# Four-row operands for small fp32 matmuls, and small steps spread between half chunks

## The reference

```
# block 1: feed-forward, then a mixer with q/k normalisation, rotary tables and attention, then feed-forward
x = x + 0.5 * ml[2] * swiglu(modulate(rms_norm(x, norm1_g), ml[0], ml[1]), ffn1_w_in, ffn1_w_out)
bg, cg, vc, q, k, v, gt = split(modulate(rms_norm(x, norm2_g), ml[3], ml[4]) @ w_in)     # the same for ctx
q, k = rms_norm(q per head, q_norm_g), rms_norm(k per head, k_norm_g)   # 8 q heads, 2 k/v heads of 128
q, k = apply_axial_rope(q), apply_axial_rope(k)                         # the 256 latent tokens
o = softmax(q @ k_all.T * 128 ** -0.5) @ v_all                          # 512 keys: 256 ctx, 256 latent
x = x + ml[5] * merge_branches(conv_branch(bg, cg, vc), o, gt, w_branch_conv, w_branch_attn, w_out)
x = x + 0.5 * ml[8] * swiglu(...); x = rms_norm(x, final_g)
# block 2, layer 0: an mLSTM of 4 heads of 256 (input and forget gates from h @ 8 columns of w_in_ab) and
# a stick-breaking attention of 8 heads of 128; layer 1: pooled windows. Each with w_in, w_out and norms.
b = cumsum(lf); W = exp(b[t] - b[s] + ic[s] - m_t); h = num / max(|den|, exp(-m_t))
```

## Time and profile before

| | |
|---|---|
| median of 3 runs | 1343.05 us (1342.46 to 1348.6) |
| profiled execution, its own time | 1343.05 us |
| its span in the trace | 1341.0 us |
| PE busy | 1304.0 us, 97% of the span |
| PE weight load (PEld) busy | 1205.3 us |
| VectorE (DVE) busy | 905.2 us, 68% |
| ScalarE (ACT) busy | 647.3 us, 48% |
| mean granted TensorE clock | 0.988 |

### The profile page before, as it was taken

How to read it: one execution, slowest core, us unless ns; L and a number is a source line. 1 busy time by engine, 2 the same in 40 slices (tenths; PEclk the granted TensorE clock), 3 DMA queues, 4 the chain that set the end, 5 groups by cost and what they waited for, 6 DMA issues and landing times. The chain is left out here.

```text
span 1341.0 us, 23443 instructions
## 1 busy us (share of the span) xinstructions
PE 1304.0 (97%) x9310; PEld 1205.3 (90%) x9310; DVE 905.2 (68%) x1462; ACT 647.3 (48%) x1025; POOL 31.4 (2%) x32
## 2 busy tenths in 40 slices
PE   5999999999999999999999999999999999999996
PEld 3688888888889999999999999989999999999996
DVE  3577875556558587755775555788887666689863
ACT  4432222222336335545465445666666765556552
POOL 0000000000020000000010000200000000100000
PEclk6999999999999999999999999999999999999998
DMA  8746556464554345444546665556555454447550
GB/s 306 261 159 202 190 189 217 160 234 161 191 182 142 111 131 168 130 149 138 181 143 193 201 194 178 165 172 176 152 152 166 133 188 152 142 129 219 188 174 32
DMA packets 201404, 229.68 MB, mean 171 GB/s; under 512 B 7120, under 2 KB 191696, under 8 KB 201296
## 3 DMA queue, kind: packets, MB, share of 16 engines
q1 hardware_dynamic: 201008, 227.90, 53.4%
q10 hardware_dynamic: 288, 0.28, 0.1%
HBM read 227.10 MB, written 1.05 MB: 170 GB/s over the span
## 5 line engine op out<-in xcount | busy, mean ns | idle before, releaser
L1038 PE MATMUL P<-XHB,WH 128*128 128x256 f32 (+1 forms) x1808 | 553.6, 306 | 7.6 <-DVE XLB L1683 3.7
L1039 PE MATMUL P<-XLB,WH 128*128 128x256 f32 (+1 forms) x1808 | 543.7, 301 | 0.0
L1040 PE MATMUL P<-XHB,WL 128*128 128x256 f32 (+1 forms) x1808 | 543.6, 301 | 0.0
L1871 DVE TENSOR_TENSOR WL<-W,WH 128x1024 fp32r<-128x1024 f32 x358 | 431.9, 1224 | 96.4 <-ACT WH L1466 96.1
L1466 ACT ACTIVATE WH<-W 128x1024 fp32r<-128x1024 f32 x358 | 369.1, 1042 | 247.2 <-PE P L1040 169.9
L1038 PEld LDWEIGHTS P<-XHB,WH 128*128 128x128 f32 x1808 | 340.6, 188 | 28.1 <-issue 7.3
L1039 PEld LDWEIGHTS P<-XLB,WH 128*128 128x128 f32 x1808 | 340.4, 188 | 15.4 <-issue 0.5
L1040 PEld LDWEIGHTS P<-XHB,WL 128*128 128x128 f32 x1808 | 340.6, 188 | 14.8
L1038 PE MATMUL P<-GH,WH 128*128 128x256 f32 (+1 forms) x372 | 121.2, 326 | 0.0
L1040 PE MATMUL P<-GH,WL 128*128 128x256 f32 (+1 forms) x372 | 120.6, 324 | 0.0
L1039 PE MATMUL P<-GL,WH 128*128 128x256 f32 (+1 forms) x372 | 120.6, 324 | 0.0
(11 more groups left out here) (305 smaller groups left out, 1811.9 us busy)
## 6 DMA issues: line engine op xcount, KB each, us to landing
W<-in_ffn_w_in SPq DMA_DIRECT2D x88, 512.0 KB, 4.9
W<-in_w_in_ab SPq DMA_DIRECT2D x72, 512.0 KB, 4.6
W<-in_w_modt SPq DMA_DIRECT2D x56, 512.0 KB, 4.0
W<-in_w_in SPq DMA_DIRECT2D x52, 512.0 KB, 3.9
W<-in_ffn_w_out SPq DMA_DIRECT2D x40, 512.0 KB, 4.7
W<-in_w_in_c SPq DMA_DIRECT2D x32, 512.0 KB, 4.3
W<-in_w_mod SPq DMA_DIRECT2D x16, 512.0 KB, 7.2
W<-in_w_out_ab SPq DMA_DIRECT2D x16, 512.0 KB, 4.4
```

The source lines that it names most:

```text
L1038: pe.matmul(o, h[:, k, c], xh[:, kk, a:b], start=kk == 0, stop=False)
L1039: pe.matmul(o, h[:, k, c], xl[:, kk, a:b], start=False, stop=False)
L1040: mm = pe.matmul(o, l[:, k, c], xh[:, kk, a:b], start=False, stop=kk == gm.nk - 1)
L1871: dve.tensor_tensor(l, a, h.bitcast(F32), ALU.subtract).then_inc(S["wl"], 1)
```

## The change

It changes the shapes of some small fp32 operands and the order of some small steps.

- Shapes: HOT is replaced by a constant `hot` of 16 columns; "qa" uses 4 columns of it (128 rows by 4 columns) and writes 4 PSUM rows; root and reciprocal work on 4 partitions. "qb" and the two `sel` matmuls of "m0" take 4 rows of `sel` and 4 rows of the moving operand. G has 4 partitions.
- GpSimd's three memsets and the semaphores `hot` and `gz`, with the waits on them, are gone.
- Order: in `qk_norm`, "qb" of tile i comes first, then a yield, then "rope" of the tile before and a yield. In `attention`, "score", "gather" and "turn" no longer stand in one tick but have a yield between them, and ScalarE's exponential is done in the "score" step, ahead of the "gather" and "turn" copies, with no step of its own.

```
-for _name, _n in (("id", 128), ("one", 128), ("eps", 1), ("ee", 1), ("gat", 2), ("cnt", 26), ("perm", 128),
+for _name, _n in (("id", 128), ("one", 128), ("eps", 1), ("ee", 1), ("hot", 16), ("gat", 2), ("cnt", 26), ("perm", 128),
...
         for i in range(4):
+            b, f = self.bank(self.up("qn"))
+            self.step("qb", a=s, b=i, c=self.at("qn"), bank=b, free=f)
+            at = self.at("qn")
+            yield
             if todo is not None:
                 self.rope(*todo)
+                yield
                 todo = None
-            b, f = self.bank(self.up("qn"))
-            self.step("qb", a=s, b=i, c=self.at("qn"), bank=b, free=f)
             if s < 2 or i % 2:
-                todo = (s, i, self.at("qn"))
+                todo = (s, i, at)
...
-            yield
-            yield
...
         score(0)
-        self.step("exp", a=0, bank=4 + (self.uses - 1) % 3)
         for i in range(16):
-            for _ in range(2):
-                yield
+            yield
+            yield
             self.step("scale", a=i)
-            for _ in range(2):
-                yield
             if i + 1 < 16:
                 while missing(i + 1):
                     yield True
                 score(i + 1)
-                bank = 4 + (self.uses - 1) % 3
+            yield
             if i and i % 2 == 0:
                 b, f = self.bank(self.up("ol"))
                 self.step("gather", a=i // 2 - 1, bank=b, free=f)
+            yield
             b, f = self.bank(self.up("at"))
             self.step("turn", a=i, bank=b, free=f)
-            if i + 1 < 16:
-                self.step("exp", a=i + 1, bank=bank)
-        for _ in range(2):
+        for _ in range(3):
             yield
...
-            G = sbuf(st, "G", [128, 6, T])
+            G = sbuf(st, "G", [4, 6, T])
...
-                        pe.matmul(ps[:, 0:T], HOT[:, 3 - i:131 - i], SQ[...], start=i == 0,
+                        pe.matmul(ps[0:4, 0:T], con("hot", 4 * i, 4 * i + 4), SQ[...], start=i == 0,
...
-                    pe.matmul(ps[:, 0:T], con("sel", 128 * s.b, 128 * s.b + 128),
+                    pe.matmul(ps[:, 0:T], con("sel", 128 * s.b, 128 * s.b + 128, 4),
                               rows_of(s.a), start=True, stop=True).then_inc(S["qb"], 1)
...
-                    pe.matmul(ps[:, 0:T], con("sel", 128 * h, 128 * h + 128), G[:, 4, 0:T], start=True, stop=True)
-                    pe.matmul(ps[:, T:2 * T], con("sel", 128 * h, 128 * h + 128), G[:, 5, 0:T], start=True,
+                    pe.matmul(ps[:, 0:T], con("sel", 128 * h, 128 * h + 128, 4), G[:, 4, 0:T], start=True, stop=True)
+                    pe.matmul(ps[:, T:2 * T], con("sel", 128 * h, 128 * h + 128, 4), G[:, 5, 0:T], start=True,
                               stop=True).then_inc(S["m1p"], 1)
...
-            pool.wait_ge(S["md"], 56)
-            pool.memset(HOT, 0.0).then_inc(S["hot"], 1)
-            pool.wait_ge(S["hot"], 1)
-            pool.memset(HOT[:, 3:4], 1.0).then_inc(S["hot"], 1)
...
-                if name == "s3":
-                    pool.wait_ge(S["oh"], 8)
-                    pool.memset(G[:, 4:6, :], 0.0).then_inc(S["gz"], 1)
...
-                    act.activation(rows_of(s.a), ps[:, 0:T], ACT.Sqrt, scale=1.0 / 128, bias=con("eps")) \
+                    act.activation(rows_of(s.a), ps[0:4, 0:T], ACT.Sqrt, scale=1.0 / 128, bias=con("eps", rows=4)) \
...
-                elif s.kind == "exp":
+                elif s.kind == "score":
                     i = s.a
                     act.wait_ge(S["am2"], i + 1)
...
-                    dve.wait_ge(S["gz"], 1)
```

More of the change, by code:

```diff
@@ L78, in constants @@
     put("ee", np.full((128, 1), EPS * EPS, np.float32))
+    hot = np.zeros((128, 4, 4), np.float32)
+    for i in range(4):
+        hot[:, i, i] = 1.0
+    put("hot", hot.reshape(128, 16))
     put("gat", (p[:, None] % 32 == np.arange(2)[None, :]).astype(np.float32))
@@ L712, in qk_norm @@
         for i in range(4):
+            b, f = self.bank(self.up("qn"))
+            self.step("qb", a=s, b=i, c=self.at("qn"), bank=b, free=f)
+            at = self.at("qn")
+            yield
             if todo is not None:
                 self.rope(*todo)
+                yield
                 todo = None
-            b, f = self.bank(self.up("qn"))
-            self.step("qb", a=s, b=i, c=self.at("qn"), bank=b, free=f)
             if s < 2 or i % 2:
-                todo = (s, i, self.at("qn"))
+                todo = (s, i, at)
             else:
                 self.ready.add(self.name(s, i))
-                self.end[self.name(s, i)] = self.at("qn")
-            yield
-            yield
+                self.end[self.name(s, i)] = at
         if todo is not None:
@@ L845, in build_program @@
         seq, stat, end = plan.seq, plan.stat, plan.end
-        names = ("g wh wl zero gz hot sc mm mr mt mv md cb sf sq pa on sr ra ri rb am gm out sil1 hm1 hh1 hl1 xu1 sil2 hm2 hh2 hl2 xu2 "
+        names = ("g wh wl zero sc mm mr mt mv md cb sf sq pa on sr ra ri rb am gm out sil1 hm1 hh1 hl1 xu1 sil2 hm2 hh2 hl2 xu2 "
                  "nt nh nl xh xr rx "
@@ L900, in build_program @@
             SM = sbuf(st, "SM", [128, 4, 4])
-        HOT = MC[:, 0, 0:131]
         with ExitStack() as st:
@@ L948, in rows_of @@
         def rows_of(s):
-            return MC[:, 7, :] if s == 2 else RS[:, 1, T * s:T * s + T]
+            return MC[0:4, 7, :] if s == 2 else RS[0:4, 1, T * s:T * s + T]
         def head(s, i):
@@ L1121, in _ @@
                 elif s.kind == "qa":
-                    pe.wait_ge(S["hot"], 2)
                     for i in range(4):
@@ L1125, in _ @@
                         pe.wait_ge(S["qs"], n + 1)
-                        pe.matmul(ps[:, 0:T], HOT[:, 3 - i:131 - i], SQ[:, n % 3, T * (n // 3 % 2):T * (n // 3 % 2) + T], start=i == 0,
+                        pe.matmul(ps[0:4, 0:T], con("hot", 4 * i, 4 * i + 4), SQ[:, n % 3, T * (n // 3 % 2):T * (n // 3 % 2) + T], start=i == 0,
                                   stop=i == 3).then_inc(S["qh"], 1)
@@ L1175, in _ @@
                     for j in range(2):
-                        mm = pe.transpose(ps[:, 4 * j:4 * j + 4], G[0:4, 2, 128 * j:128 + 128 * j], con("id", 0, 4, 4))
+                        mm = pe.transpose(ps[:, 4 * j:4 * j + 4], G[:, 2, 128 * j:128 + 128 * j], con("id", 0, 4, 4))
                     mm.then_inc(S["gmm"], 1)
@@ L1570, in _ @@
                 elif s.kind == "g1":
-                    t2 = G[0:4, 2, 0:T]
+                    t2 = G[:, 2, 0:T]
                     act.wait_ge(S["gfree"], 1)
-                    act.activation(t2, G[0:4, 1, 0:T], ACT.Abs).then_inc(S["gab"], 1)
+                    act.activation(t2, G[:, 1, 0:T], ACT.Abs).then_inc(S["gab"], 1)
                     act.wait_ge(S["gab"], 1)
@@ L2073, in _ @@
                     dve.wait_ge(S["gr0"], 1)
-                    dve.tensor_scalar(G[0:4, 0, 0:T], TS[0:4, 5, 0:T], V[0:4, VEC["bi"][0]:VEC["bi"][1]], None, ALU.add) \
+                    dve.tensor_scalar(G[:, 0, 0:T], TS[0:4, 5, 0:T], V[0:4, VEC["bi"][0]:VEC["bi"][1]], None, ALU.add) \
                         .then_inc(S["gr0"], 1)
@@ L2077, in _ @@
                     dve.wait_ge(S["gmm"], 1)
-                    dve.tensor_scalar(G[0:4, 1, 0:T], ps[0:4, T:2 * T], V[0:4, VEC["bf"][0]:VEC["bf"][1]], None, ALU.add) \
+                    dve.tensor_scalar(G[:, 1, 0:T], ps[0:4, T:2 * T], V[0:4, VEC["bf"][0]:VEC["bf"][1]], None, ALU.add) \
                         .then_inc(S["gfree"], 1)
                 elif s.kind == "g2":
-                    ig, b, t2, top, neg = (G[0:4, i, 0:T] for i in range(5))
+                    ig, b, t2, top, neg = (G[:, i, 0:T] for i in range(5))
                     dve.wait_ge(S["gfree"], 1)
@@ L2099, in _ @@
                     dve.wait_ge(S["dv"], own)
-                    dve.tensor_tensor(G[0:4, 5, 0:T], neg, b, ALU.subtract).then_inc(S["gq"], 1)
+                    dve.tensor_tensor(G[:, 5, 0:T], neg, b, ALU.subtract).then_inc(S["gq"], 1)
                 elif s.kind == "g4":
```

## The result

| | before | after |
|---|---|---|
| median of 11 runs each, in turn on one chip | 1348.05 us | 1357.49 us |
| lowest and highest | 1341.86, 1355.03 | 1349.24, 1362.73 |
| profiled execution, its own time | 1343.05 | 1357.65 |
| its span | 1341.0 | 1355.9 |

The ratio is 1.0067, with a 95% interval of 1.0043 to 1.0092, or +5.8 to +12.4 us. The forecast was a ratio of 1349.0/1343.05 = 1.0044, at the lower edge of that. The time lies above the range of 1342.5 to 1353.0. The runs of either kernel scatter over 13 us. The three runs known when the prediction was made had shown 6 of these.

What follows compares the result with a forecast made beforehand. TensorE was taken as the bound, with no idle time in q/k normalisation and attention. Four-row visits at "qb" (4.7) and "m0" (1.2) sum to +5.9 us, all else 0: 1343.05 + 5.9 = 1349.0 us, range 1342.5 to 1353.

Steps and rivals of the forecast that it cites:

- A visit to four rows: TensorE at 12 "qb" and the "m0" of heads 1 to 3: 0.39 us each, +5.9 us in sum.
- four rows cost nothing: Rival, chance 0.16: the 15 four-row visits at "qb" and "m0" cost 0, time 1343.0 us, not slower.
- unhidden second loads: Rival case at "qb" and "m0": second-pass loads unhidden too, 8.2 us, 1351.3; shares a 0.20 chance with the long step.
- "m0" of head 0: mLSTM stage, right behind four-row "g4": the way back only moves behind "m0", so 0.
- "qa", 0: q/k normalisation: going from 128 to 4 columns costs 0, as at "gr"; upper bound 0.8 us for three visits.
- Memsets and constants, 0: GpSimd's memsets are covered by other work, and constants grow by only 64 bytes a partition: 0.
- The order, 0 on TensorE: `qk_norm` and `attention`: with weights three chunks ahead, TensorE never sees ScalarE's extra stops: 0; late splits 0 to 3 us.
- a late split: Rival, chance 0.06: ScalarE's stop at "score" makes weights late, 16 tiles, up to 0.2 us each: 1352, slower.
- The spacing, 0 with bounds of 3 either way: Matmul stream between 425 and 680 us: flips between short and long step cancel, 0, bounds -3 to +3 us.
- The base, 1343.05 us: Profiled execution of the kernel before, also its median then, to which the forecast added its +5.9 us.
- The long step as well: Rival, chance 0.20 shared with unhidden loads: visits cost 5.9, attention's matmuls take the long step, +3.2: 1352.2 us.

Runs made afterwards that it cites:

- dose4: Kernel before plus 96 extra lone products of 256 columns on 4 rows in the mixer's second half: 1425.36 us, ratio 1.0594.
- dose128: Kernel before plus 96 extra lone products of 256 columns on 128 rows in the mixer's second half: 1392.03 us, ratio 1.0348.
- shapes_only: Kernel before with the change's 4-row and 4-column operands and no memsets, in the old order: 1347.92 us, ratio 1.0021.
- order_only: Kernel before with the change's new order of yields alone, old shapes: 1352.02 us, ratio 1.0041.
- the first probe: First of ten extra products in the second feed-forward: 1356.33 us on the kernel before (1356.03 with varied widths), 1355.61 on the changed kernel.

## Why the prediction was right in its sign and short in its size

In short: the price of four rows was right, and three terms put at 0 were not. Four columns were priced by the wrong row (0.9 us), the new order by the wrong queue (0.8), and the two steps of the stream only where the edits are. And the base of 1343.05 us was one of several times that the kernel before takes: 5.0 us of the 8.5 between the forecast and the result.

**A visit to four rows, 0.39 us: right**, as a size and as a sum. 12 "qb" cost 4.7 us and three "m0" 1.2, and dose4 against dose128 gives the same price 96 times. The reading of "g1" (the way in 0.1 late, the way back 0.1 late, and on each way a load of 128 columns, 0.11, no longer hidden) was all of it. What it left out is that "m0" has waits behind it, which took back 0.5 of the 1.2. With it the rival "four rows cost nothing" falls, and so does that of unhidden second loads (0.50 a visit).

**"m0" of head 0, 0: short by 0.1.** The way back did move behind the "m0", as said, and takes an unhidden load with it, that of the q k product. But the first load of "m0" itself, which was unhidden as part of the way back before, stays so behind the short "g4" (load at 935.68, first pass 0.14 us later).

**"qa", 0: wrong.** Each of the three visits cost 0.29, 0.9 us in all, just above the 0.8 that the prediction gave as the upper bound. The step that failed is the choice between two rows: "gr" has the same number of rows and near the same number of columns, "g1" and "qa" share the fp32 type, and I went by the shape. At "gr" I also read the way in alone; its way back is behind a wait and shows nothing.

**Memsets and constants, 0**: no run undid these alone, and shapes_only, which drops them too, can't bound them, since steps worth several microseconds moved both ways in it.

**The order, 0 on TensorE: wrong, 0.8 us by waits.** I looked at ScalarE's stops and at how far ahead the splits are; that lead did hold (ScalarE waits for TensorE for 48.2 us at line 1458, where it was 48.4). What came late is VectorE's scaling, which has no such lead: "scale" stands two ticks ahead of its "turn", as before, and a tick is 12 matmuls, 1.4 us, while the work ahead of it in VectorE's queue is 4.7 us long here (544.21 to 548.89). The prediction compared the lead with that of before, and not with what else is in that queue at the new place. It foresaw for the order "0 to 3 us", by a late split; the size fits, the cause was another. Both waits are in order_only, none in shapes_only.

**The spacing, 0 with bounds of 3 either way: the mechanism right, its reach wrong.** The prediction saw a step of two sizes which "holds until some small product comes, and then may flip", and priced it only between 425 and 680 us. There it came out as about +1.3 (within the bounds). But in the second feed-forward 1578 matmuls stand in one unbroken stretch, and there the profiled execution of the changed kernel has the long step: 6.8 us, more than everything that the change does to "qb". Nothing in the prediction's own argument confined the flip to the stages with edited steps; the bound should have been taken over every stretch, the longest above all. That the change causes this flip isn't shown. The steps ahead of the first edited product and ahead of the first probe came out both ways too.

**The base, 1343.05 us: the larger part of the miss.** Against the comparison's own median, 1348.05, the forecast of +5.9 gives 1354.0, and 1357.49 was measured, 3.5 more. 1.8 of these are "qa", "turn" and the "m0" of head 0; the other 1.7 are less than the width of the interval (+5.8 to +12.4) can tell.

The times of both kernels lie in three groups with nothing between them:

| 11 runs each, us | lowest group | middle | highest |
|---|---|---|---|
| before | 1341.9 to 1343.1 (5) | 1348.1 to 1350.3 (4) | 1353.5, 1355.0 |
| after | 1349.2 to 1351.9 (4) | 1356.9 to 1359.1 (5) | 1362.6, 1362.7 |

The 44 runs of the changed kernel on record and 23 further ones of the kernel before fall into the same three groups, all at granted clocks of 0.988 to 0.990. From group to group, by the medians of the table's runs, the change costs 8.1, 8.6 and 8.4 us. The two profiled executions are of different groups, 1343.05 and 1357.65; their 14.9 us less the 6.8 of the second feed-forward are 8.1 too. So the change costs some 8 us, not 15: the 7.2 of marks and waits, and about 1 of steps. That the groups are flips of the two longest stretches is likely. Their flips are worth 6.8 and 4.8 us, and the groups lie 7 and 5 apart. But each kernel was traced in one group alone, so this stays argued, and so does how much of the median's +9.4 us is the second feed-forward.

**The long step as well**, the rival with 0.20, comes nearest to what happened: in the attention it came by +1.9 of the 3.2 us that it said, and in the profiled execution in another stage as well. It gave 1352.2.

## What to carry to other kernels

A small fp32 product with up to 64 rows, or up to 64 columns of weights, between full 128x128 ones isn't a cheap one: its stream is as long, its load is no longer hidden, and it pays to enter and to leave. When the engine is the bottleneck, pad it with zeros to 128 rows and columns, as this kernel did before, or put such products side by side, so that one visit serves all of them. When small steps are spread out, read the queue of every engine that feeds them and not only of the one that waits first; and before a gain or a loss under 1% is put down to an edit, count the matmuls per window in the stretches that the edit doesn't touch, and take enough runs of both kernels to see whether their times fall into groups.

## What the runs showed of the hardware

- The price of few rows has an edge: 4, 32 and 64 rows cost 0.39 us a visit for a product of 256 columns, 96 and 128 cost none. Numbers between 64 and 96 were not run.
- Few columns cost about the same for fp32 (0.29 to 0.34 us for 4, 8, 32 and 64), while fp32r with 8 columns behind fp32r products costs nothing on the way in (0.12 from start to start at "gr"); its way back is hidden by a wait here.
- The fp32r stream of 128x128 by 128x256 runs at 0.1133 or 0.1178 us a matmul at the same granted clock of 1.00 and the same DMA share of 0.60, for over a thousand matmuls at a time. A small product or its width can switch it, either way. The same work ahead of a stretch doesn't fix it, and the times of one and the same program fall into groups 5 to 7 us apart.
